# Two-block transformer step: inverse head norms by Ln and Exp on ScalarE, head sums one turn ahead, VectorE's work around merge and w_out in another order

## What is computed

```python
q = (_rms(c_q, g_q_latent) @ w_uq).reshape(B, S, 8, 192)
kv = (_rms(c_kv, g_kv_latent) @ w_ukv).reshape(B, S, 8, 256)
k_nope, v = kv[..., :128], kv[..., 128:]
k = concat([k_nope, k_pe_h])                  # 128 + 64, k_pe shared by the heads
q, k = _rms(q, g_q_head), _rms(k, g_k_head)   # x * rsqrt(mean(x*x) + 1e-6) * g, per head
# rope on the last 64 of q and k
y_a = causal softmax attention(q, k, v)       # 8 heads, two query blocks of 128
merged = sigmoid(gl_a) * (y_a @ w_proj_mla) + sigmoid(gl_b) * (y_b @ w_proj_sb)
x = x + gt1 * (merged @ w_out)
x = x + gt2 * FFN(modulated rms norm of x)
```

## Time and profile before

| | us |
|---|---|
| median of 3 runs | 2635.07 (2633.29 to 2635.34) |
| the profiled execution | 2635.05 |
| its span | 2633.4 |
| PE busy | 2513.3 (95%) |
| DVE busy | 1805.9 (69%) |
| ACT busy | 1080.1 (41%) |
| mean granted TensorE clock | 0.982 |
| first logits of the turns to the first matmul of the projection of `y_a` | 1633.73 to 1735.08 |
| third sub of w_out to its eleventh | 1794.21 to 1824.18 |

### The profile page before, as it was taken

One profiled execution on the slowest core, in us unless ns is written; L12 is line 12 of the kernel. 1 busy time (PEld: TensorE's weight loads), 2 busy tenths in 40 slices (PEclk: granted clock), 3 DMA queues, 4 the chain that ended last, 5 costly groups with the idle time before them and its releaser, 6 DMA issues.

```text
span 2633.4 us, 33569 instructions
## 1 busy us (share of the span) xinstructions
PE 2513.3 (95%) x13086; PEld 2121.3 (81%) x13086; DVE 1805.9 (69%) x1774; ACT 1080.1 (41%) x1244; POOL 222.2 (8%) x397
## 2 busy tenths in 40 slices
PE   4869999999999999999999998898999999999999
PEld 3659547888888888889999997787888888888887
DVE  6866766887888888678675446865678655555565
ACT  2025105444334344464336555444543344444443
POOL 4411220111111111001110000000001000000000
PEclk8889999999999999999999999999999999999999
DMA  9988895888888888648875554244578655555554
GB/s 367 366 318 295 310 384 175 313 327 319 314 308 318 307 313 293 197 159 292 310 270 162 162 170 132 81 144 151 201 259 307 218 190 189 189 189 189 187 191 144
DMA packets 290569, 638.97 MB, mean 243 GB/s; under 512 B 21754, under 2 KB 34556, under 8 KB 290076
## 3 DMA queue, kind: packets, MB, share of 16 engines
q1 hardware_dynamic: 233808, 432.22, 48.4%
q0 software_dynamic: 56096, 205.02, 21.0%
q10 hardware_dynamic: 556, 0.18, 0.0%
HBM read 635.28 MB, written 2.10 MB: 242 GB/s over the span
## 4 chain that ended last, share of the span: by engine, by line
PE 83%; DVE 8%; DMA 4%; issue 2%; ACT 2%; POOL 0%; DVEq 0%; ACTq 0%; POOLq 0%
PE PS L1627 82%; DMA R<-in_w_ada 4%; DVE R L973 2%; DVE WLO L954 1%; ACT WHI L511 1%; DVE R L1521 1%; PE PS L1848 1%; PE PS L1769 0%; DVE R L1349 0%; ACT R L584 0%; DVE R L1047 0%; DVE R L1590 0%; DVE YF L1592 0%; DVE R L1374 0%; DVE H L1120 0%
## 5 line engine op out<-in xcount | busy, mean ns | idle before, releaser
L954 DVE TENSOR_TENSOR WLO<-RAW,WHI 128x1024 fp32r<-128x1024 f32 x760 | 929.2, 1225 | 683.3 <-ACT WHI L511 681.0
L511 ACT ACTIVATE WHI<-RAW 128x1024 fp32r<-128x1024 f32 x760 | 804.3, 1060 | 1150.1 <-PE PS L1627 1146.5
L1627 PE MATMUL PS<-WHI,H 128*128 128x512 f32 x3296 | 1027.8, 393 | 32.3 <-issue 18.9
L1627 PEld LDWEIGHTS PS<-WHI,H 128*128 128x128 f32 x3296 | 618.4, 189 | 164.8 <-issue 28.5
L1627 PE MATMUL PS<-WLO,H 128*128 128x512 f32 x1648 | 645.0, 391 | 0.0
L973 DVE SCALAR_TENSOR_TENSOR R<-R,CA 128x1024 f32<-128x1024 f32 x360 | 461.3, 1281 | 70.4 <-DMA R<-in_w_ada 63.2
L1627 PE MATMUL PS<-H,WHI 128*128 128x256 f32 x2656 | 490.9, 287 | 12.8 <-DVE WLO L954 11.7
L1627 PEld LDWEIGHTS PS<-H,WHI 128*128 128x128 f32 x2656 | 417.8, 193 | 19.1 <-DVE WLO L954 16.4
L1627 PE MATMUL PS<-WHI,HID 128*128 128x512 f32 x1280 | 395.8, 390 | 0.0
L1627 PE MATMUL PS<-H,WLO 128*128 128x256 f32 x1328 | 377.6, 284 | 0.0
L1627 PEld LDWEIGHTS PS<-WLO,H 128*128 128x128 f32 x1648 | 311.5, 189 | 65.9
(11 more groups left out here) (215 smaller groups left out, 1266.7 us busy)
## 6 DMA issues: line engine op xcount, KB each, us to landing
R<-in_w_ada POOLq DMA_DIRECT2D x384, 512.0 KB, 6.6
RAW<-in_w_in SPq DMA_DIRECT2D x88, 1024.0 KB, 5.9
RAW<-in_w_ffn_in SPq DMA_DIRECT2D x88, 1024.0 KB, 5.0
RAW<-in_w_ffn_gate SPq DMA_DIRECT2D x44, 1024.0 KB, 6.3
RAW<-in_w_ffn_up SPq DMA_DIRECT2D x44, 1024.0 KB, 5.2
RAW<-in_w_ffn_down SPq DMA_DIRECT2D x44, 1024.0 KB, 8.2
RAW<-in_w_ffn_out SPq DMA_DIRECT2D x44, 1024.0 KB, 5.1
RAW<-in_w_out SPq DMA_DIRECT2D x32, 1024.0 KB, 5.1
```

The lines of the kernel that those rows point to most:

```text
L511: nc.scalar.activation(WHI[j][:, :, :], RAW[slot][:, 2 * half:2 * half + 2, :], ACT.Copy)\
L954: nc.vector.tensor_tensor(WLO[j][:, :, :], RAW[slot][:, 2 * half:2 * half + 2, :], WHI[j][:, :, :].bitcast(F32), ALU.subtract).then_inc(lo ...
L1627: return nc.tensor.matmul(o, a, b, start=start, stop=stop, skip_group_check=True)
```

## The change

Head norms: the mean, the root and the reciprocal go. In their place `head_inverse` on ACT takes the logarithm of sum / 192 + epsilon straight out of PSUM pair C (epsilon comes from a column `TINY` that DVE sets in the first half of the block) and then the exponential of -0.5 times that. It waits until the previous pair's inverse norms have been used (`hd_scaled`), since the tiles are the same.

```diff
-            def head_roots(hp):
+            def head_inverse(hp):
+                act.wait_ge(hd_ss, hp + 1)
+                if hp:
+                    act.wait_ge(hd_scaled, hp)
+                nc.scalar.activation(tiles(73, 4), flat("C"), ACT.Ln, bias=TINY, scale=1.0 / 192).then_inc(hd_ms, 1)
                 act.wait_ge(hd_ms, hp + 1)
-                nc.scalar.activation(tiles(73, 4), tiles(73, 4), ACT.Sqrt).then_inc(hd_rt, 1)
+                nc.scalar.activation(tiles(73, 4), tiles(73, 4), ACT.Exp, scale=-0.5).then_inc(hd_rt, 1)
...
             for n in range(7):
+                if n == 6:
+                    head_inverse(1)
                 hi(2)
                 copy_out(LAT[n][0], tiles(LAT[n][1], 4))
...
                 if n == 4:
-                    head_roots(0)
+                    head_inverse(0)
+                    head_squares(1)
...
             for hp in range(4):
-                if hp < 3:
-                    head_squares(hp + 1)
-                    head_roots(hp + 1)
+                if hp < 2:
+                    head_squares(hp + 2)
...
-                hi(2)
+                hi(3)
                 act.wait_ge(pt_mm, hp + 1)
                 nc.scalar.activation(SC, PAIR["B"][:, :, 0:384], ACT.Copy).then_inc(pt_ev, 1)
-                hi(2)
+                hi()
+                if hp < 2:
+                    head_inverse(hp + 2)
```

```diff
                 if n == 5:
                     swaps(0)
+                    head_sums(1)
...
                 if hp < 3:
-                    head_sums(hp + 1)
                     swaps(hp + 1)
                     pe.wait_ge(hd_ms, hp + 2)
...
                 ins.then_inc(pt_mm, 1)
+                if hp < 2:
+                    head_sums(hp + 2)
                 pe.wait_ge(pt_ev, hp + 1)
```

```diff
-                if hp < 3:
-                    head_means(hp + 1)
-                    head_reciprocals(hp + 1)
+                if hp < 2:
+                    rope_gains(hp + 2)
                 lo(2)
...
                 if hp < 3:
-                    heads_scaled(hp + 1)
+                    nope_scaled(hp + 1)
+                merge_b(hp)
+                if hp < 3:
+                    rope_scaled(hp + 1)
                 lo(2)
-                merge_b(hp)
```

```diff
             merge_a(3)
-            split(2, first=0)
-            diagonals(2, mod_at(1, 2))
+            lo()
+            split(1, first=0)
+            lo()
+            split(1, first=1)
             for g in range(4):
                 for s in range(8):
-                    if g or s >= 2:
+                    if g or s >= 4:
                         lo()
+                    if g == 0 and s >= 4:
+                        diagonals(2, mod_at(1, 2), (s - 4,))
...
-                rows = {2: 0, 4: 1, 6: 2, 8: 3}
+                rows = {6: 0, 7: 1, 8: 2, 9: 3}
```

More of the change, by code:

```diff
@@ L244, in build @@
         RS1, TOTAL = SM[:, 48:50], SM[:, 56:58]
+        TINY = SM[:, 63:64]
         SUMS = SS.rearrange("p (g t n) -> p g t n", g=2, t=2)
@@ L798, in w_out_squares @@
                     for s in range(8):
-                        if g or s >= 2:
+                        if g or s >= 4:
                             hi()
[L801 to L804, removed]
+                        if g == 0 and s == 7:
+                            gate_row(k, 0)
+                        if g == 1 and s in (0, 1, 2):
+                            gate_row(k, s + 1)
                         if g and s == 4:
@@ L931, in _ @@
             hi(2)
-            split([(free["A"], A_LAT + 2), (free["B"], B_LAT + 2)], first=0)
+            split([(free["A"], A_LAT + 2)], first=0)
+            hi()
+            split([(free["B"], B_LAT + 2)], first=1)
+            hi()
             w_out_squares(2, 8)
@@ L1040, in split_affine, with diagonals @@
                                         H[:, 4 * q:4 * q + 4, 0:T].bitcast(F32), ALU.subtract).then_inc(h_quad, 1)
-            def diagonals(k, gate):
+            def diagonals(k, gate, quads=range(4)):
                 if k:
                     dve.wait_ge(gt_mm, 4 * k)
-                for t in range(KT):
+                for t in (4 * q + i for q in quads for i in range(4)):
                     ins = nc.vector.tensor_scalar(DIAG[:, t, :], ident, MOD[:, gate + t:gate + t + 1], None, ALU.mult)
@@ L1423, in _ @@
                 if s == 8:
+                    step(nc.vector.memset(TINY, EPS))
                     dve.wait_ge(lat_ss, 2)
@@ L1500, in merge_b @@
             def merge_b(g):
-                dve.wait_ge(pe_sub, c.sub.value(-2))
+                dve.wait_ge(pe_sub, c.sub.value())
                 nc.vector.tensor_tensor(tiles(48 + 4 * g, 4), flat("C"), tiles(48 + 4 * g, 4), ALU.mult)\
@@ L1507, in _, with rope_gains @@
             col = lambda name: PRM[:, COL[name]:COL[name] + 1]
-            def head_means(hp):
-                dve.wait_ge(hd_ss, hp + 1)
-                nc.vector.tensor_scalar(tiles(73, 4), flat("C"), 1.0 / 192, EPS, ALU.mult, ALU.add).then_inc(hd_ms, 1)
+            def rope_gains(hp):
+                dve.wait_ge(hd_sq, 1 + 3 * (hp + 1))
                 if hp == 0:
@@ L1517, in head_means, with nope_scaled @@
                     .then_inc(rope_in, 1)
-            def head_reciprocals(hp):
+            def nope_scaled(hp):
                 dve.wait_ge(hd_rt, hp + 1)
-                step(nc.vector.reciprocal(tiles(73, 4), tiles(73, 4)))
-            def heads_scaled(hp):
                 for a in range(2):
@@ L1528, in heads_scaled, with rope_scaled @@
                                                    R[:, 75 + a, :], ALU.mult, ALU.mult)
+            def rope_scaled(hp):
                 dve.wait_ge(rope_swap, hp + 2)
@@ L1544, in _ @@
             for n in range(7):
+                if n == 5:
+                    nope_scaled(0)
                 lo(2)
@@ L1550, in _ @@
                 if n == 4:
-                    head_means(0)
-                    head_reciprocals(0)
+                    rope_gains(0)
                 if n == 5:
-                    heads_scaled(0)
+                    rope_scaled(0)
+            rope_gains(1)
             for hp in range(4):
@@ L1586, in merge_a @@
             def merge_a(n):
-                dve.wait_ge(pe_sub, c.sub.value(-2))
+                dve.wait_ge(pe_sub, 2 * U_PROJ + 16 + 4 * (n + 1))
                 pair, g = "AB"[n % 2], MERGED[n]
@@ L2055, in head_sums @@
                 pe.wait_ge(free["C"], C_LAT + max(hp - 1, 0))
+                if hp == 1:
+                    pe.wait_ge(hd_ms, 1)
                 for n, (nope, rope, half) in enumerate(((78, 80, EVEN), (79, 80, ODD), (81, 77, EVEN), (82, 77, EVEN))):
```

## The result

The changed kernel takes 2605.12 us (median of 4 runs, 2604.10 to 2606.92) against 2635.20 before: a ratio of 0.9889, 95% interval 0.9878 to 0.9901. The forecast was 2609 us with a range of 2604 to 2616. The profiled execution is the longest of the four, 2606.92 us (span 2605.2); against the 2635.05 of the kernel before that is 28.1 us, where the prediction had 26.2.

What follows compares the result with a forecast made beforehand. It took the bound to be the stretches where the chain of waits leaves PE: entry to the turns, each turn's root chain, entry to w_out. 17.3 + 8.9 = 26.2 off 2635.05 gave 2609 us, range 2604 to 2616.

Steps and rivals of the forecast that it cites:

- PE no longer waits for a root: In the turns: pair h+2's inverse root is made in turn h, from sums PE makes after that turn's transposes.
- Ln and Exp: On ACT, per pair: logarithm, exponential and a table load before each, 4.6 us; bounds 2.3 and 4.6.
- one load for the pair: Skill's rule on ACT tables: stretch before logits 0 up to 2.6 us shorter, whole 2606 us; rows side against it.
- the drain: Skill's 1.38 us added to each ACT table load; twice on the stretch before logits 0 would give 2612.
- Entry: Before the pair turns: logits 0 start at 1632.9 against 1633.73, waiting for ACT's copy; gain 0.8 us.
- Low clock at the first logits: In logits 0, after a PE pause of 4.6 us: 2.8 us lost, bounds 0 and 3.
- Turns: Four head-pair turns of 21.7, 21.7, 19.75 and 18.9 us; next stage at 1717.75 instead of 1735.08, 17.3 us gained.
- w_out: Entry to w_out: third sub 5.5 us earlier, third to eleventh sub 3.4 us shorter; 8.9 us, bounds 4 and 9.5.
- A: Rival: the pause before logits 0 leaves no low clock; 2606 us, chance 0.10.
- B: Rival: ACT becomes the late engine in turns 0 and 1, or w_out gives 4 of 8.9; 2614, chance 0.12.
- C: Rival: nothing is left, since PE was waiting for weights all along; 2635 us, chance 0.03.
- D: Rival, slower: PE stays at 1.2 GHz through the turns, +84 against 26 saved; 2693 us, chance 0.03.

Runs made afterwards that it cites:

- e4_ln_old_order: Kernel before, with logarithm and exponential on ACT replacing mean, root and reciprocal, everything in the old order: 2615.70 us, ratio 0.9926.
- e6_identity_for_ln: Changed kernel with Identity in place of the logarithm, so norms are not computed and seven of eight table loads go: 2602.04 us.
- e11_changed_again: The changed kernel unaltered, run again beside the kernel with four moves on one chip: 2606.25 us, ratio 0.9892.
- e10_warm_pause: Changed kernel with 36 transposes of the identity on PE in the pause before the first logits: 2602.77 and 2607.89 us.
- e9_entry_only: Changed kernel with pair 1's head sums behind the last latent product and ACT's copy ahead of pair 1's root: 2599.09 and 2607.32 us.
- the kernel with four moves: Changed kernel: pair 1's sums after the last latent product, ACT's copy before its root, turn 2's rope before merge_b, H's split in turn 3: 2599.57 us.

## Why the prediction was right

- **Bound and mechanism.** The chain that was read, root, reciprocal, low part, was the bound of the turns; taking it out gave what the list of durations said. That in this kernel it is the function and not the order that pays was not said in the prediction; it gave the head sums' place the credit ("PE no longer waits for a root"), and `e4_ln_old_order` shows that 18.2 of the 19 us come without it. What the new order gains in the turns (131.63 - 48.20 against 132.19 - 41.98, 6.8 us) it loses again ahead of the first logits (6.2 us). So the total came out right, and how it divides between function and order the prediction did not say.
- **Ln and Exp** at 4.6 us: measured 1.28 + 1.11 + 1.28 + 1.06 = 4.8 with the gaps. Where it is waited for, before the first logits, `e6_identity_for_ln` priced the loads at 2.55. The sentence on one load for the pair, drawn from the Trainium skill (ScalarE: Activation LUTs, Table sets: the hidden batching unit), does not hold in this kernel: each of the four `L889` and four `L891` has its load. Nor does the trace show the drain that the Trainium skill (ScalarE: Activation LUTs, What ACT_TABLE_LOAD costs) adds to a load: the activation starts 0.01 us behind it.
- **Entry: 0.8 us.** Measured 0.81. ACT's queue behind the rope was the limit, as reckoned.
- **Low clock at the first logits: 2.8 us.** This is the term that was mis-sized: 1.65 (4.53 against 2.87). The low stretch ended while the logits ran, and they took 4.53 us; in another execution of the same kernel (`e11_changed_again`) it cost 1.95. The price of the earlier trace rows was taken for a constant, and it is not.
- **Turns: 21.7, 21.7, 19.75, 18.9.** Measured 21.57, 21.59, and 38.3 for the last two against 38.65.
- **w_out: 8.9.** Measured 9.46. The start of the third sub gained 5.5 us as forecast; third to eleventh sub took 25.6 us and not 26.6, since a gate row was put at 1.1 us with its pause and takes 0.8 without; and 0.4 us behind the eleventh sub, for which the prediction has nothing, went the other way.
- **Sum.** 1.15 + 0.25 + 0.35 + 0.56 make 2.3 us more than forecast, less 0.4 us by which the profiled execution came late to the stretch: 28.1 against 26.2. So 2 us of the 4 by which 2609 missed the median are terms of the sum, and they all erred to one side. The other 1.8 us, between its 2606.92 and the median, are the spread of the runs, which the prediction did not allow for when it took the profiled execution for the median.
- **Rivals.** A (no low clock) did not come in the changed kernel but is what `e6_identity_for_ln` and `e10_warm_pause` show: 1.6 us, not 2.8. B fell: ACT was reckoned to have 0.8 us to spare in a turn, and the trace has 0.93 us of idle time there. C and D fell: the clock was at 1.00 in turns 1 to 3. D's germ is real all the same: with the reciprocal back, a low stretch came in each of three turns, and PE was busy 5.1 us longer.

## What to carry to other kernels

Before moving a long operation, ask what stands behind it on its engine in every place it could go: 6.5 us on an engine that feeds PE two buffers ahead hurt in both orders, and replacing it by two short ones on an idle engine gave 18 us with no reordering. The order was worth 6.6 us more only when the entry was put right. So look at the entry of a pipeline by itself: work pulled a turn ahead has to be done before the first turn too, and there it stood in front of the one copy that everything waited for.

## What was not expected of the hardware

- Table loads of 1.28 us that stand in an idle stretch of ACT cost nothing: two fewer in each of turns 0 and 1 left them at 21.58 us.
- Transposes of the identity in a pause kept the clock, in the one trace with them: behind 36 of them in 3.93 us it stayed at 1.00, and the 16 logits took 2.87 us instead of 4.53.
- The length of a pause does not tell whether the clock falls to 1.2 GHz: 2.10 and 2.89 us did it, 2.10 in another kernel and 2.33 did not.
- The same kernel varies by 3 to 8 us from run to run (2630.03 to 2637.23 before, 2599.09 and 2607.32 for `e9_entry_only`). Of the two traces of the kernel with four moves, 3.1 us apart, all of that lies ahead of the first low part; from there to the projection they agree to 0.02 us. Where the clock falls at another moment, as in the two traces of the changed kernel, it is 0.36 us.
